# Exponentials one step later on ScalarE, softmax factors one step later on VectorE, in a two-layer attention kernel

## The chip, the cores and the metric

The kernel runs on one core of one Trainium2 chip. The metric is the device time of one execution in microseconds (us). The time before is 1312.04 us, the median of three runs (1309.96 to 1312.55).

## The reference, cut to what matters

Two layers, 512 tokens, width 1024, all in float32. Each layer runs two kinds of attention on the same normalised input, projects the joined result back and adds it, and then runs a feed-forward part with a short convolution:

```python
for l in range(DEPTH):                                   # 2 layers
    proj = rms_norm(x, attn_norm[l]) @ w_in[l]
    q_lat, kv_lat, k_rope, nsa_q, nsa_kv, gate_logits = jnp.split(proj, SPLIT_POINTS, axis=-1)
    o_mla = mla_attention(...)      # 8 heads, causal softmax
    o_nsa = nsa_attention(...)      # 8 heads, three gated branches:
                                    # compressed keys, selected keys, window
    x = x + jnp.concatenate([o_mla, o_nsa], axis=-1) @ w_out[l]
    x = x + conv_ffn(rms_norm(x, ffn_norm[l]), ...)
return rms_norm(x, final_norm)
```

The heart of each attention is `softmax(q k^T + mask) v`. With 512 tokens the selected and the window branch both come down to a causal softmax over all earlier tokens; the compressed branch is a small softmax over 31 pooled keys.

## The kernel before, in words

Every engine has its own program, with the order written out by hand, and semaphores tie the programs together. A layer is input projection, attention, output projection, feed-forward. The change is in the attention stage, which runs from about 104 to 250 us in layer 1 and from about 750 to 895 us in layer 2 of the profiled execution.

The stage is cut into 48 **units**: a unit is one block of 128 queries for one pair of heads and one branch. Four units (the blocks 2, 3, 0, 1, so with 384, 512, 128 and 256 keys) make a **group** g; groups 0 to 3 are the first kind of attention, 4 to 11 the second (its matmuls are L1631 and L1632, those of the first kind L1626). All engines walk through steps s = 0, 1, 2, ... and work on unit s - something in step s:

- TensorE in step s: transposes of the probabilities of unit s-3 (`turn`, L1645); then, in every fourth step, `spread(g)` (L1659), the transposes of the factors of group g, in step 4g+7; then the scores of unit s; in odd steps the products with the values for two units (L1692); and items from other work, among them `compressed` (L1704).
- VectorE in step s: adds the mask, takes the row maxima and writes the masked scores to SBUF (`row_max(s)`, L1193); the one-over-sum factors of a group (`factors(g)`, L1199, then L1204 or with gates L1208), in step 4g+5; the copy of the spread factors (`copy_factors`, L1219) in step 4g+7; `normalize` (L1226, L1230); `out_lo` (L1234); the low halves of other items (`item_lo`, L1245 and L1247), of the compressed branch (L1306 to L1320, L1261, L1267) and of the weights of the output projection (`split_lo`, L578) in steps 33, 37, 41 and 45.
- ScalarE in step s: copies unit s-3's transposed probabilities from PSUM to SBUF (`evac_turn`, L881 and L884 for the large blocks, L888 for the small); the exponentials of unit s (`exps(s)`, two activations of L870, each with the read of its sum); then other items: `evac_out` (L895), `item_hi` (L904 to L911), pieces of the compressed branch (L935 to L953, of which L938 and L949 wait for GpSimd) and the high halves of weights (`split_hi`, L571) in steps 32, 36, 40 and 44.

The transposes of the probabilities go to two PSUM banks in turn (3 and 4; from step 29 on also bank 5), and a large block takes both. So TensorE can transpose the next block only once ScalarE has copied the one before. TensorE's `turn(u)` waits for `exp_done` of unit u and for the copy that frees its bank; `spread(g)` waits for `fac_ready`, which `factors(g)` signals; `factors(g)` waits for the last exponentials of its group, unit 4g+3. `row_max(u)` waits until unit u-3 has been transposed, since three buffers hold the probabilities. The order within a step is what sets who waits behind whom:

```python
# ScalarE, L920 to L923
if 0 <= s - T_LAG < U: evac_turn(s - T_LAG)     # T_LAG = 3
if s < U: exps(s)
# VectorE, L1290 to L1296
if s < U: row_max(s)
if 0 <= s - 2 < U and (s - 2) % T == T - 1: factors((s - 2) // T)
```

Of the kernel before, what the change touches and what calls it, by code (L numbers as in the profile page):

```python
# [36 lines left out]
T = S // P  # L37
# [33 lines left out]
U = U_MLA + U_NSA  # L71
# [98 lines left out]
def at(s, l, n):  # L170

    return l * PER_LAYER[s.name] + (n + CREDIT.get(s.name, 0))
# [74 lines left out]
def hybrid_layers(nc, a, out):  # L247

    with ExitStack() as ctx:
# [337 lines left out]
        def unit(u):  # L587

            i, n = ORDER[u % T], u // T
            if u < U_MLA:  # L590
                return i, n, 0
            n -= U_MLA // T
            return i, H // 2 + n // 2, n % 2
# [151 lines left out]
        def _(act):  # L745
# [30 lines left out]
            for l in range(L):  # L776
# [78 lines left out]
                def evac_proj(kind, n, bank):  # L855

                    if kind == "k":
                        k_rows(n, bank)
                    if kind == "v":
                        v_rows(n, bank)  # L860
# [4 lines left out]
                def exps(u):  # L865
                    n = (unit(u)[0] + 1) * P
                    for h in range(2):
                        row = probs[:, u % 3, h, 0:n]
                        act.wait_ge(max_done, at(max_done, l, 2 * u + h + 1))
                        activate(row, row, ACT.Exp, scale=-1.0, bias=nmax[:, u % 4, h:h + 1],  # L870
                                 accum_out=rsum[:, u // T % 2, unit(u)[0], h:h + 1]).then_inc(exp_done, 1)
# [44 lines left out]
                for s in range(U + LAG + 2):  # L916
                    if s < len(STEP_PROJ):
                        for job in STEP_PROJ[s]:
                            evac_proj(*job)
                    if 0 <= s - T_LAG < U:  # L920
                        evac_turn(s - T_LAG)
                    if s < U:
                        exps(s)  # L923
                    if s == 2:
                        act.wait_ge(gate_in, at(gate_in, l, 1))
                        activate(gates[:, :, :], gate_e[:, :, :], ACT.Exp, scale=-1.0).then_inc(gate_exp, 1)
                    g = (s - LAG - 1) // T
                    if s > LAG and (s - LAG - 1) % T == T - 1:
                        if g < H // 2:
                            evac_out(g)  # L930
                    if s in ITEM_STEP:
                        item_hi(ITEM_STEP.index(s))
                    if s == HID_STEP:
                        act.wait_ge(cmp_used, at(cmp_used, l, 4))
                        activate(hid_rows, ps[:, HID_BANK, 0:CHID], ACT.Copy).then_inc(hid_out, 1)  # L935
                    if s == HIDT_STEP + 1:
                        act.wait_ge(gelu_in, at(gelu_in, l, 1))
                        activate(gelu_t, gelu_t, ACT.Exp, scale=-2.0 * (2.0 / np.pi) ** 0.5).then_inc(gelu_exp, 1)  # L938
                    if s == KVC_STEP:
                        act.wait_ge(kvc_acc, at(kvc_acc, l, 1))  # L940
                        activate(kc[:, :, :], ps[:, KVC_BANK, S - G * NCP:S].rearrange("p (g c) -> p g c", g=G), ACT.Copy)\
                            .then_inc(kch_done, 1)
                    if s in CS_STEP:
                        g = CS_STEP.index(s)
                        act.wait_ge(cs_acc, at(cs_acc, l, g + 1))
                        activate(cs_t[g], ps[:, CS_BANK[g], :], ACT.Copy).then_inc(cs_out, 1)
                    if s == CS_MAX_STEP + 1:
                        act.wait_ge(cs_sub, at(cs_sub, l, 1))
                        activate(scp, scp, ACT.Exp).then_inc(cs_exp, 1)  # L949
                    if s in PC_STEP:  # L950
                        g = PC_STEP.index(s)
                        act.wait_ge(pc_tp, at(pc_tp, l, g + 1))
                        activate(pct[:, g, :], ps[:, PC_BANK, :], ACT.Copy).then_inc(pct_ready, 1)  # L953
                    if s in WOUT_STEP:
                        split_hi(act, l, POS_WOUT + WOUT_STEP.index(s))
# [82 lines left out]
        def _(dve):  # L1038
# [47 lines left out]
            for l in range(L):  # L1086
# [129 lines left out]
                def copy_factors(g):  # L1216

                    dve.wait_ge(fac_done, at(fac_done, l, g + 1))
                    v.tensor_copy(onorm[:, g % 2, :], ps[:, FAC_BANK[g][0], :]).then_inc(fac_out, 1)  # L1219
# [61 lines left out]
                for s in range(U + LAG + 2):  # L1281
                    done = (s - LAG - 2) // T
                    closed = s >= LAG + 2 and (s - LAG - 2) % T == T - 1
                    if closed and done < H // 2:
                        out_lo(done)
                    if s > LAG + U_MLA and (s - LAG - 1 - U_MLA) % (2 * T) == 2 * T - 1:
                        add_compressed((s - LAG - 1 - U_MLA) // (2 * T))
                    if LAG <= s < U + LAG and (s - LAG) % T == T - 1:
                        copy_factors((s - LAG) // T)
                    if s < U:  # L1290
                        row_max(s)
                    if s < len(STEP_PROJ):
                        for job in STEP_PROJ[s]:
                            evac_proj(*job)
                    if 0 <= s - 2 < U and (s - 2) % T == T - 1:
                        factors((s - 2) // T)  # L1296
                    if s > LAG and (s - LAG - 1) % T == T - 1:
                        normalize((s - LAG - 1) // T)
                    if closed and done >= H // 2 and done % 2 == 1:
                        out_lo(H // 2 + (done - H // 2) // 2)  # L1300
                    if s - 1 in ITEM_STEP:
                        item_lo(ITEM_STEP.index(s - 1))
                    if s == HIDT_STEP + 1:
                        dve.wait_ge(hid_tp, at(hid_tp, l, 1))
                        pos = ps[:, HIDT_BANK, 0:2 * CMP_COLS].rearrange("p (a c) -> p a c", a=2)[:, :, 2 * NC]
                        tt(hid_b[:, :], pos, cols[:, C_B1:C_B1 + 2], ALU.add).then_inc(dve_chain, 1)  # L1306
                        dve.wait_ge(dve_chain, ch.next())
                        for kv in range(2):
                            c = kv * CMP_COLS
                            last = v.tensor_scalar(hid[:, kv, :, 0:NC],  # L1310
                                                   ps[:, HIDT_BANK, c:c + G * NC].rearrange("p (g c) -> p g c", g=G),
                                                   hid_b[:, kv:kv + 1], None, ALU.add)
                        last.then_inc(hid_in, 1)
                    if s == HIDT_STEP + 2:
                        dve.wait_ge(gelu_exp, at(gelu_exp, l, 1))
                        v.tensor_scalar(gelu_t, gelu_t, 1.0, None, ALU.add).then_inc(dve_chain, 1)
                        dve.wait_ge(dve_chain, ch.next())
                        v.reciprocal(gelu_t, gelu_t).then_inc(dve_chain, 1)
                        dve.wait_ge(dve_chain, ch.next())
                        tt(hid_flat, hid_flat, gelu_t, ALU.mult).then_inc(hid_ready, 1)  # L1320
                    if s == KVC_STEP + 1:
                        dve.wait_ge(kch_done, at(kch_done, l, 1))
                        v.tensor_copy(v_cmp[:, :, :], ps[:, KVC_BANK, 0:G * HD].rearrange("p (g c) -> p g c", g=G))\
                            .then_inc(kvc_ready, 1)
                    if s - 1 in BACK_STEP:
                        cs_mask(BACK_STEP.index(s - 1))
                    if s == CS_MAX_STEP:
                        cs_less_max()
                    if s == CS_SCALE_STEP:
                        cs_scale()  # L1330
                    if s == 3:
                        dve.wait_ge(gate_exp, at(gate_exp, l, 1))
                        v.tensor_scalar(gates[:, :, :], gates[:, :, :], 1.0, None, ALU.add).then_inc(dve_chain, 1)
                        dve.wait_ge(dve_chain, ch.next())
                        v.reciprocal(gates[:, :, :], gates[:, :, :]).then_inc(gates_ready, 1)
                    if s - 1 in WOUT_STEP:
                        split_lo(dve, l, POS_WOUT + WOUT_STEP.index(s - 1))
# [659 lines left out]
```

## Time and profile before

| | |
|---|---|
| median of 3 runs | 1312.04 us |
| the profiled execution's own time | 1311.85 us |
| its span, first to last instruction | 1310.1 us |
| TensorE matmuls busy | 1267.1 us, 97% |
| TensorE weight loads busy | 1045.5 us, 80% |
| VectorE busy | 700.1 us, 53% |
| ScalarE busy | 639.3 us, 49% |
| mean granted TensorE clock | 0.994 |

Busy times are sums over the instructions of an engine. Matmuls are pipelined and their ends are modelled, so a busy share of 97% is not a TensorE at its peak; where TensorE shows as idle, it was waiting. The clock is given as a share of full speed. The chain of work that ended last is 85% TensorE, 8% VectorE and 4% ScalarE.

### The profile page before, as it was taken

How to read it: one execution, taken by the hardware profiler on the slowest of the kernel's cores; microseconds unless marked ns; L12 is line 12 of the kernel's file. 1: busy time of each engine (PE TensorE's matmuls, PEld its weight loads, DVE VectorE, ACT ScalarE, POOL GpSimd, SP SyncE). 2: the span in 40 equal slices, each digit the busy share in tenths (PEclk: the TensorE clock that was granted, in tenths of full speed). 3: DMA queues.
4: the chain of work that ended last, by engine and by line, in shares of the span. 5: the costliest groups of instructions: out<-in, count | busy, mean ns of one | idle time of the engine just before them, and what ended most of it. 6: DMA issues, size and time to landing. Idle time of an engine off the chain costs nothing.

```text
span 1310.1 us, 18479 instructions
## 1 busy us (share of the span) xinstructions
PE 1267.1 (97%) x6612; PEld 1045.5 (80%) x6612; DVE 700.1 (53%) x1216; ACT 639.3 (49%) x1191; POOL 70.7 (5%) x161
## 2 busy tenths in 40 slices
PE   8999989999999999999999999899999999999997
PEld 7997667788888888888889866667888888888886
DVE  5435778455555555533363457782655555554334
ACT  4336788344444444322352468782454444443223
POOL 2013110000000000000010311100000000000000
PEclk9999999999999999999999999999999999999999
DMA  6420101124333333332143210012223333333211
GB/s 205 125 89 1 66 1 49 42 72 120 97 96 99 97 97 99 105 98 97 45 121 94 65 65 1 1 57 86 76 75 97 97 97 96 98 105 114 96 64 65
DMA packets 121003, 107.05 MB, mean 82 GB/s; under 512 B 3763, under 2 KB 110485, under 8 KB 120946
## 3 DMA queue, kind: packets, MB, share of 16 engines
q1 hardware_dynamic: 118912, 101.13, 25.3%
q0 software_dynamic: 1456, 3.52, 0.9%
q10 hardware_dynamic: 578, 1.64, 0.3%
q8 instruction: 35, 0.57, 0.2%
q14 instruction: 22, 0.18, 0.0%
HBM read 104.19 MB, written 2.10 MB: 81 GB/s over the span
## 4 chain that ended last, share of the span: by engine, by line
PE 85%; DVE 8%; ACT 4%; issue 2%; POOL 1%; DMA 1%; DVEq 0%; ACTq 0%; POOLq 0%
PE ps L1449 24%; PE ps L1451 24%; PE ps L1450 24%; PE ps L1645 3%; PE ps L1692 3%; DVE probs L1193 2%; PE ps L1626 2%; ACT probs L870 1%; PE ps L1632 1%; PE ps L1631 1%; DVE probs L1066 1%; DVE w_lo L578 1%; DVE x L1084 1%; PE ps L1659 1%; PE ps L1704 1%
## 5 line engine op out<-in xcount | busy, mean ns | idle before, releaser
L1449 PE MATMUL ps<-ht_hi,w_hi 128*128 128x512 f32 (+2 forms) x776 | 297.2, 383 | 2.5 <-DVE w_lo L578 2.5
L1451 PE MATMUL ps<-ht_hi,w_lo 128*128 128x512 f32 (+2 forms) x776 | 295.9, 381 | 0.0
L1450 PE MATMUL ps<-ht_lo,w_hi 128*128 128x512 f32 (+2 forms) x776 | 295.8, 381 | 0.0
L578 DVE TENSOR_TENSOR w_lo<-raw,w_hi 128x1024 fp32r<-128x1024 f32 (+4 forms) x196 | 218.7, 1140 | 95.0 <-ACT w_hi L571 86.7
L571 ACT ACTIVATE w_hi<-raw 128x1024 fp32r<-128x1024 f32 (+4 forms) x196 | 187.2, 982 | 107.9 <-PE ps L1451 107.6
L1365 DVE SCALAR_TENSOR_TENSOR conv<-ps,cols,conv 128x510 f32<-128x510 f32 (+1 forms) x176 | 127.6, 746 | 179.7 <-ACT conv L978 173.9
L1449 PEld LDWEIGHTS ps<-ht_hi,w_hi 128*128 128x128 f32 x776 | 145.9, 188 | 30.8 <-DVE w_lo L578 3.0
L1450 PEld LDWEIGHTS ps<-ht_lo,w_hi 128*128 128x128 f32 x776 | 145.9, 188 | 28.0 <-issue 0.5
L1451 PEld LDWEIGHTS ps<-ht_hi,w_lo 128*128 128x128 f32 x776 | 145.9, 188 | 27.8
L1449 PE MATMUL ps<-w_hi,ht_hi 128*128 128x430 f32 (+1 forms) x392 | 147.3, 376 | 3.7 <-DVE w_lo L578 2.0
L978 ACT ACTIVATE conv<-ps,cols 128x512 f32<-128x512 f32 x88 | 68.1, 774 | 159.9 <-PE ps L1451 159.7
L1451 PE MATMUL ps<-w_hi,ht_lo 128*128 128x430 f32 (+1 forms) x392 | 144.5, 369 | 0.0
L1450 PE MATMUL ps<-w_lo,ht_hi 128*128 128x430 f32 (+1 forms) x392 | 144.4, 368 | 0.0
L1449 PE MATMUL ps<-w_hi,g_hi 128*128 128x512 f32 x352 | 137.2, 390 | 0.8 <-DVE g_all L1373 0.8
L1450 PE MATMUL ps<-w_lo,g_hi 128*128 128x512 f32 x352 | 137.0, 389 | 0.0
L1451 PE MATMUL ps<-w_hi,g_lo 128*128 128x512 f32 x352 | 136.9, 389 | 0.0
L870 ACT ACTIVATE probs<-probs,nmax 128x384 f32<-128x384 f32 (+1 forms) x192 | 106.2, 556 | 31.1 <-DVE nmax L1193 30.5
L1193 DVE CUSTOM_DVE_ANT_0 probs<-ps,causal 128x384 f32<-128x384 f32 (+1 forms) x192 | 87.1, 487 | 50.2 <-PE ps L1626 25.0
L997 ACT ACTIVATE g_hi<-g_all 128x512 fp32r (+1 forms) x44 | 27.6, 630 | 149.8 <-PE ps L1451 149.8
L1386 DVE TENSOR_TENSOR g_lo<-g_all,g_hi 128x512 fp32r<-128x512 f32 x44 | 30.3, 691 | 129.8 <-ACT g_hi L997 129.8
L1645 PE MATMUL ps<-ident,probs 128*128 128x128 f32 x480 | 72.5, 278 | 21.6 <-ACT probs_t L881 12.0
L1449 PEld LDWEIGHTS ps<-w_hi,ht_hi 128*128 128x128 f32 x392 | 73.9, 189 | 12.2 <-DVE w_lo L578 2.6
(193 smaller groups left out, 1510.7 us busy)
## 6 DMA issues: line engine op xcount, KB each, us to landing
raw<-in_ffn_w_up_dram SPq DMA_DIRECT2D x88, 512.0 KB, 4.1
raw<-in_ffn_w_down_dram SPq DMA_DIRECT2D x44, 512.0 KB, 3.3
raw<-in_w_in_dram SPq DMA_DIRECT2D x32, 430.0 KB, 4.3
raw<-in_w_out_dram SPq DMA_DIRECT2D x16, 512.0 KB, 3.4
raw<-in_nsa_cmp_w_dram SPq DMA_DIRECT2D x8, 512.0 KB, 3.7
x<-in_x_dram ACTq DMA_DIRECT2D x3, 512.0 KB, 8.1
raw<-in_mla_w_uq_dram SPq DMA_DIRECT2D x4, 384.0 KB, 2.9
out_dram<-x SPq DMA_DIRECT2D x3, 512.0 KB, 2.6
```

The source lines that it names most:

```text
L571: last = nc.scalar.activation(d(w_hi)[:, :, d0:d1], r(raw)[:, :, r0:r1], ACT.Copy)
L578: last = nc.vector.tensor_tensor(d(w_lo)[:, :, d0:d1], r(raw)[:, :, r0:r1], d(w_hi)[:, :, d0:d1].bitcast(F32), ALU.subtract)
L870: activate(row, row, ACT.Exp, scale=-1.0, bias=nmax[:, u % 4, h:h + 1], accum_out=rsum[:, u // T % 2, unit(u)[0], h:h + 1]).then_inc(exp_d ...
L978: activate(conv[:, fl, uv, :], ps[:, 4 * fl + uv, :], ACT.Identity, bias=bias, scale=tap)\
L1193: v.tensor_tensor_reduce(probs[:, u % 3, h, 0:n], score_place(u, h), causal[:, S - n:S], -1.0, -NEG, ALU.add, ALU.min, nmax[:, u % 4, h:h ...
L1365: ins = stt(out=conv[:, fl, uv, back:S], in0=ps[:, 4 * fl + uv, 0:S - back], scalar=c, in1=conv[:, fl, uv, back:S], op0=ALU.mult, op1=ALU.add)
L1386: tt(g_lo[:, n % 2, :].unsqueeze(1), g_all[:, bass.ds(k, 1), :], g_hi[:, n % 2, :].unsqueeze(1).bitcast(F32), ALU.subtract).then_inc(gl_do ...
L1449: mm(o, lhs[0], rhs[0], start=start, stop=False)
L1450: mm(o, lhs[0], rhs[1], start=False, stop=False)
L1451: return mm(o, lhs[1], rhs[0], start=False, stop=stop)
L1645: last = nc.tensor.transpose(ps[:, bank, c0 + b * P:c0 + (b + 1) * P], probs[:, u % 3, h, b * P:(b + 1) * P], ident[:, :])
L1692: last = mm(ps[64 * h:64 * h + VD, out_bank(g), q0 + q:q0 + 2 * P], w, pt_half(u)[:, h, b, q:2 * P], start=b == 0, stop=b == n - 1)
```

## The change

ScalarE runs the exponentials of unit s-1 in step s, where it ran those of unit s; they still come behind that step's copy of transposed probabilities. The pass through step 48 takes in the last unit. VectorE's factors of a group move from step 4g+5, behind the row maxima, to step 4g+6, ahead of them, since the exponentials that they wait for now come a step later.

```diff
@@ ScalarE, the loop over steps
                     if 0 <= s - T_LAG < U:
                         evac_turn(s - T_LAG)
-                    if s < U:
-                        exps(s)
+                    if 1 <= s <= U:
+                        exps(s - 1)
                     if s == 2:
@@ VectorE, the loop over steps
                     if LAG <= s < U + LAG and (s - LAG) % T == T - 1:
                         copy_factors((s - LAG) // T)
+                    if 0 <= s - 3 < U and (s - 3) % T == T - 1:
+                        factors((s - 3) // T)
                     if s < U:
                         row_max(s)
                     if s < len(STEP_PROJ):
                         for job in STEP_PROJ[s]:
                             evac_proj(*job)
-                    if 0 <= s - 2 < U and (s - 2) % T == T - 1:
-                        factors((s - 2) // T)
```

## Rows read from the trace of the kernel before

**Rows 1.** Waits, layer 1's attention: who waited; us in total, times, longest

```profile
PE ps L1645 <- ACT probs_t L881: 6.0, 5, 2.6
PE ps L1645 <- ACT probs_t L888: 4.8, 4, 2.4
...
PE ps L1847 <- DVE qs L1247: 0.5, 1, 0.5
```

**Rows 2.** Timeline of TensorE: start, length, work, idle before it and its releaser

```profile
142.13 0.52 PE L1645 MATMUL ps<-ident,probs 128*128 128x128 f32 x3 [2.37 <-ACT probs_t L888]
...
182.91 1.06 PE L1645 MATMUL ps<-ident,probs 128*128 128x128 f32 x8 [2.58 <-ACT probs_t L881]
...
219.39 0.63 PE L1645 MATMUL ps<-ident,probs 128*128 128x128 f32 x4 [0.81 <-ACT probs_t L881]
...
237.31 1.06 PE L1645 MATMUL ps<-ident,probs 128*128 128x128 f32 x8 [1.39 <-ACT probs_t L881]
```

**Rows 3.** Timeline of ScalarE, exponentials of 512 and of 128 keys

```profile
214.59 0.72 ACT L870 ACTIVATE probs<-probs,nmax 128x512 f32<-128x512 f32 x1
...
217.99 0.40 ACT L870 ACTIVATE probs<-probs,nmax 128x128 f32<-128x128 f32 x1 [1.40 <-DVE nmax L1193]
```

**Rows 4.** Timeline of VectorE, ends of groups 6, 7 and 8

```profile
198.39 0.69 DVE L1208 TENSOR_TENSOR onorm<-fac,gates 128x512 f32<-128x512 f32 x1
...
205.60 0.69 DVE L1208 TENSOR_TENSOR onorm<-fac,gates 128x512 f32<-128x512 f32 x1
...
215.31 0.69 DVE L1208 TENSOR_TENSOR onorm<-fac,gates 128x512 f32<-128x512 f32 x1
215.93 0.68 DVE L1234 TENSOR_TENSOR ht_lo<-onorm,ht_hi 128x512 fp32r<-128x512 f32 x1
216.53 1.22 DVE L578 TENSOR_TENSOR w_lo<-raw,w_hi 128x1024 fp32r<-128x1024 f32 x1
217.66 0.28 DVE L1193 CUSTOM_DVE_ANT_0 probs<-ps,causal 128x128 f32<-128x128 f32 x1
```

**Rows 5.** Timeline of TensorE, the spreads of groups 6, 7 and 8

```profile
199.14 0.66 PE L1659 MATMUL ps<-ident,onorm 128*128 128x128 f32 x4
...
207.10 0.60 PE L1659 MATMUL ps<-ident,onorm 128*128 128x128 f32 x4
...
216.06 0.66 PE L1659 MATMUL ps<-ident,onorm 128*128 128x128 f32 x4
```

**Rows 6.** Timeline of VectorE, factors of group 1 and what follows them

```profile
137.43 0.20 DVE L1199 RECIPROCAL fac<-rsum 128x8 f32<-128x8 f32 x1
...
138.00 0.15 DVE L1306 TENSOR_TENSOR hid_b<-ps,cols 128x2 f32<-128x2 f32 x1
```

**Rows 7.** Timeline, the compressed branch's chain in steps 21 to 23

```profile
176.45 0.20 DVE L1199 RECIPROCAL fac<-rsum 128x8 f32<-128x8 f32 x1
...
177.29 0.68 DVE L1261 TENSOR_TENSOR vm<-ps,cmask 128x512 f32<-128x512 f32 x1
178.01 1.22 DVE L1267 TENSOR_REDUCE cstat<-vm 128x32 f32<-128x1024 f32 x1
...
179.38 1.91 POOL L726 TENSOR_TENSOR vm<-vm,cstat 128x1024 f32<-128x1024 f32 x1 [8.81 <-DVE cstat L1267]
...
181.33 1.06 ACT L949 ACTIVATE vm<-vm 128x1024 f32<-128x1024 f32 x1 [0.98 <-POOL vm L726]
```

**Rows 8.** Windows: stretch, length, busy TensorE, loads, VectorE, ScalarE, GpSimd, then granted clock

```profile
144.00:145.00 1.00, 1.00 (x5) 0.51 (x6) 0.86 (x4) 0.74 (x3) 0.00 (x0) 0.50 0.00 0
...
831.00:832.00 1.00, 1.00 (x4) 0.80 (x3) 0.79 (x3) 1.00 (x5) 0.95 (x1) 0.50 0.00 0
```

**Rows 9.** Timeline of TensorE, the same work in layer 1 and layer 2

```profile
187.68 0.66 PE L1864 MATMUL ps<-ident,vm 128*128 128x128 f32 x4
...
828.37 1.06 PE L1645 MATMUL ps<-ident,probs 128*128 128x128 f32 x8 [2.58 <-ACT probs_t L881]
...
834.41 0.65 PE L1864 MATMUL ps<-ident,vm 128*128 128x128 f32 x4
```

## The prediction

> **What bounds the kernel now.** I read the share of busy time first: TensorE stands at 97% of the span, so the change can only win time in which TensorE waits. The chain that ended last says the same (85% TensorE). Then I looked for the waits in the attention stage, since the diff touches nothing else. The reader should see that in layer 1's stage TensorE waits 11.3 us in ten places, and that nine of them, 10.8 us, end on ScalarE's copies L881 and L888; the tenth is VectorE's L1247 [rows 1]. The timeline gives the places: one of 2.37, one of 2.58, one of 0.81, one of 1.39 [rows 2]. Layer 2 repeats them (its 2.58 stands in [rows 9]). So some 22 us of 1310 are the most that ScalarE's order could be worth. What keeps a copy late is seen on ScalarE's own timeline: in step 38 it sat 1.40 us until VectorE had the maxima of the unit whose exponentials stood first [rows 3]. The copy of step 39, which TensorE wanted at 218.6, stood behind them.
>
> **ScalarE's part.** Nothing is added: 192 activations of L870 stay, each group of exponentials is only taken one place later, when its maxima are long there. That removes the wait of [rows 3] and its like. The price is slack: turn(u) on TensorE then finds its exponentials one step instead of two steps old. Four steps of TensorE are 8.96 us (207.10 to 216.06) [rows 5], 2.2 a step, and the two largest exponentials are 0.72 each [rows 3], so I cost it at nothing; if ScalarE were full it would be a wait of up to 1.4. The two waits in the second half of a stage, 0.81 and 1.39 idle, go [rows 2]. I take 1.0 and 1.5 for them, since a gap is longer than its idle by the end of a pipelined matmul; **-2.5 a layer**.
>
> **Waits that stay.** The 2.37 is not ScalarE's order: the copy stands behind L938, which waits for GpSimd, which waits for VectorE's L1310. The 2.58 is the same with L949 [rows 2, 7]. There the other half of the diff helps. In step 9 factors(1) ran ahead of L1306 and took 0.57 [rows 6]; it now comes behind, so that chain is 0.6 earlier. The 0.5 on L1247 goes in the same way, as its step 13 has factors too [rows 1]. So TensorE and all behind it is 1.1 early at step 21. There factors(4) took 0.84 between the maxima and the sum and maximum of the compressed branch (176.45 to 177.29) [rows 7], and it leaves too; about 0.2 more comes from the copy L895 that VectorE waited for. The chain L1267, GpSimd's L726, ScalarE's L949, copy L881 [rows 7] is therefore 2.1 early, and with it the transposes at 182.91 [rows 2]: **-2.1 a layer**. The small waits of L888 and L881 between do go, but nothing is added for them: GpSimd's chain sets the time of 182.91 whatever TensorE does before it.
>
> **VectorE's part, the cost.** In the second half of the stage factors(g) moves from behind the maxima of step 4g+5 to the start of step 4g+6. In the text of the loop it also moves behind everything else of step 4g+5: out_lo, 0.60 (215.93 to 216.53), and split_lo, 1.13 (216.53 to 217.66) [rows 4]. TensorE's spread(g) in step 4g+7 waits for it, and the two rows show how close: for group 6 L1208 ends at 198.39 + 0.69 = 199.08 and the spread starts at 199.14, slack none; for group 8 it is 216.00 against 216.06, slack none; for group 7 206.29 against 207.10, slack 0.75 after a latency of 0.06 [rows 4, 5]. So:
> - group 6, step 29 has out_lo alone: +0.60
> - group 7, step 33 has split_lo alone: 1.13 - 0.75 = +0.38
> - group 8, step 37 has both: 0.60 + 1.13 = +1.73
> - groups 9 and 10 repeat 7 and 8: +0.38, +1.73
>
> Sum **+4.8 a layer**. VectorE's work here is timed by TensorE's scores a few steps earlier, so an early stage moves both and the slack stays. Queued behind the factors on VectorE is only row_max(4g+6), whose start does not change in these groups. The wait of spread(g) holds up the scores behind it by as much. The copy L1219 comes later with it, and only normalize(g) needs that, in the next step.
>
> **The clock.** In layer 2 TensorE's granted clock fell to 0.50, the 1.2 GHz level, for some 3 us after the gap of 2.58 [rows 8, 9]. The same work, from the transposes after the gap to L1864, took 4.77 us in layer 1 (182.91 to 187.68), where the clock held, and 6.04 in layer 2 (828.37 to 834.41) [rows 2, 9]: a fall costs 1.27. There are three falls in the two stages, the others after the gap of 2.37 in each layer (that of layer 1 is in [rows 8]). A fall after a gap depends on more than its length, as these two of 2.58 show. Bounds: all three go, -3.8; none goes and the four new gaps of 1.7 each bring one, +5.1. Gaps up to 1.39 brought none [rows 2]. I take one fall gone, that of layer 2's 2.58, since that gap is cut up: **-1.3**.
> The Trainium skill (TensorE: Matmul & The Clock Gate, A second HAM failure mode: psum-queue depth-cycling) says that frequent short idles between groups of matmuls can themselves make the clock swing between its levels. By that rule the new short gaps would cost as well, which is the rival on the slow side below; the trace, with its gaps of 0.81 and 1.39 at full clock, so far speaks against it.
>
> **Sum.** Per layer -2.5 - 2.1 + 4.8 = +0.2, two layers +0.4, clock -1.3: 1311.85 - 0.9 = 1310.95 against the profiled execution. That execution lies 0.2 under the median of 1312.04, so I say 1311.2. The ends: every hand-off above is good to 0.5 a layer in the chain of GpSimd and 0.2 in the spreads; with that alone 1309.5 to 1313.8. A measurement of this kernel can tell about 0.2%, 2.6 us.
>
> **Rivals.**
> - B, all three falls of the clock go: the gaps of 2.37 and 2.58 become about 1.8 and 1.0, and near these the trace shows none. 1312.04 + 0.4 - 3.8 = 1308.6. Against it: the gap at step 23 may only be cut in two. 22%.
> - C, the spreads cost nothing, since VectorE gets through its step sooner than I think and TensorE comes later: -2.5 - 2.1 a layer and -1.3 for the clock, 1312.04 - 9.2 - 1.3 = 1301.5. Against it: slack none in two of three rows. 8%.
> - D, slower: TensorE's clock. Each new gap of 1.7 before the spreads of groups 8 and 10, in both layers, is followed by a fall, and no old one goes: 1312.04 + 0.4 + 4 x 1.27 = 1317.5. It decides from the second new fall on. For it: one gap of 2.58 had a fall and one had not. Against: 1.39 never had. 14%.
> - E, the half of the diff on ScalarE doesn't do what it says where it matters most: L895 or the chain over GpSimd waits for VectorE as late as before, the transposes at 182.91 stay where they are, and the cost of the spreads is all there: 2 x (4.8 - 2.5) = +4.6, 1316.6. For it: L895 now stands where no exponential covers its wait for normalize. 10%.
> - My case A: 46%.
>
> **How the numbers follow.** Of A's 46%, 5 lie under 1309.4, 2 over 1314.7. Faster: 22 + 8 + 5 = 35%. Slower: 14 + 10 + 2 = 26%. Within 0.2%: 39%. The range 1306.0 to 1317.0 takes in A, B and E and a part of D; A's own is 1309.5 to 1313.8.
>
> **What would show it.** Right: ScalarE's idle before L870 that L1193 ends falls to a few tenths a group; the waits of L1645 on L881 and L888 in the second half of the stage are gone; L1659 or its weight load now waits for VectorE's L1208, in groups 8 and 10 by some 1.5 us, in 4 as well; L938 and L949 still wait for GpSimd, the one 0.6 and the other some 2 us earlier. Wrong: if L1659 shows no wait, C holds; if the granted clock is at half after such a wait, D; if the transposes after L949 come no earlier, E. The feed-forward part and the projections should not move by themselves at all.

## Result, and the profile after

| | median | runs | ratio to before, 95% interval |
|---|---|---|---|
| before | 1311.18 us | 15, 1309.56 to 1312.90 | |
| after | 1315.60 us | 15, 1312.48 to 1318.78 | 1.0035 [1.0028, 1.0042] |

The change costs 4.4 us, where 0.8 was forecast as a gain (against the median of 1312.04 shown then) and no measurable difference as the likeliest. The profiled execution after has a span of 1316.9 us and an own time of 1318.78, the slowest of its 15 runs, so its span is not set against that of before. It is read below by stretches of its stage.

The page of the kernel after, shares and the costliest groups (busy time, mean ns of one | idle of the engine before them, and what ended most of it):

```profile
PE 1273.6 (97%) x6612; PEld 1050.8 (80%) x6612; DVE 702.9 (53%) x1216; ACT 637.9 (48%) x1191; POOL 72.2 (5%) x161
...
L870 ACT ACTIVATE probs<-probs,nmax 128x384 f32<-128x384 f32 (+1 forms) x192 | 105.8, 557 | 0.4
...
L1645 PE MATMUL ps<-ident,probs 128*128 128x128 f32 x480 | 73.2, 282 | 8.4 <-ACT probs_t L888 6.1
```

TensorE is as much the bound as before. ScalarE no longer waits ahead of an exponential: 0.4 us in the whole program, the 1.40 of [rows 3] is gone. That half of the change did what it says. The waits in layer 1's attention, kernel after (who waited for whom: us in total, times, longest), answer to [rows 1]:

```profile
PEld ps L1659 <- DVE onorm L1208: 7.1, 6, 1.9
PE ps L1659 <- DVE onorm L1208: 5.7, 6, 1.6
...
PE ps L1645 <- ACT probs_t L888: 3.0, 2, 2.2
ACT vm L949 <- POOL vm L726: 2.6, 1, 2.6
ACT ht_hi L895 <- DVE onorm L1226: 2.3, 3, 0.9
...
PE ps L1645 <- ACT probs_t L881: 1.6, 3, 0.9
PE ps L1659 <- DVE onorm L1204: 1.6, 1, 1.6
```

L1645's waits on ScalarE's copies fell from 10.8 us to 4.6. In their place stand waits that the kernel before did not have: the spreads L1659 on VectorE's factors, 5.7 + 1.6 = 7.3 us. The timeline of TensorE after, layer 1 (start, length, work, idle before it and what ended it), has them one by one and answers to [rows 2, 5]:

```profile
168.34 0.66 PE L1659 MATMUL ps<-ident,onorm 128*128 128x128 f32 x4 [1.55 <-DVE onorm L1204]
...
179.24 0.66 PE L1659 MATMUL ps<-ident,onorm 128*128 128x128 f32 x4 [1.59 <-DVE onorm L1208]
...
182.57 1.94 PE L1645 MATMUL ps<-ident,probs 128*128 128x128 f32 x8 [0.86 <-ACT probs_t L881]
...
193.11 1.07 PE L1704 MATMUL ps<-vm,v_cmp 32*64 32x512 f32 x4 [0.24 <-ACT vm L953]
...
201.67 0.66 PE L1659 MATMUL ps<-ident,onorm 128*128 128x128 f32 x4 [0.48 <-DVE onorm L1208]
...
210.01 0.66 PE L1659 MATMUL ps<-ident,onorm 128*128 128x128 f32 x4 [0.21 <-DVE onorm L1208]
...
220.77 0.66 PE L1659 MATMUL ps<-ident,onorm 128*128 128x128 f32 x4 [1.62 <-DVE onorm L1208]
...
229.11 0.66 PE L1659 MATMUL ps<-ident,onorm 128*128 128x128 f32 x4 [0.21 <-DVE onorm L1208]
...
239.87 0.66 PE L1659 MATMUL ps<-ident,onorm 128*128 128x128 f32 x4 [1.62 <-DVE onorm L1208]
```

The last five are spread(6) to spread(10), which the forecast had priced. The first two are spread(3) and spread(4), which it had not; it named a wait in group 4 among its signs, and none in group 3. The transposes at 182.57 are only 0.34 earlier than before, where 2.1 was forecast. Why spread(3) waits is seen on VectorE and GpSimd. The kernel before:

```profile
166.55 0.43 DVE L1204 COPY onorm<-fac 128x512 f32<-128x512 f32 x1
166.89 1.38 DVE L1245 TENSOR_TENSOR ks<-ps,ks 64x512 fp32r<-64x512 f32 x2
```

and the kernel after (VectorE, with GpSimd's row between):

```profile
165.42 1.39 DVE L1245 TENSOR_TENSOR ks<-ps,ks 64x512 fp32r<-64x512 f32 x2
166.84 0.20 DVE L1199 RECIPROCAL fac<-rsum 128x8 f32<-128x8 f32 x1
...
166.97 2.21 POOL L718 CAST ks<-ks 64x1024 fp32r<-64x1024 f32 x2 [23.80 <-DVE ks L1245]
...
167.08 1.21 DVE L1204 COPY onorm<-fac 128x512 f32<-128x512 f32 x1
```

The factors of group 3 now stand behind item_lo (L1245, 1.39), and they land beside the cast L718 that item_lo has just released on GpSimd: the same copy takes 1.21 instead of 0.43. It ends at 168.29, and the spread starts at 168.34.

**Stretches.** From here the stage is measured from spread to spread on TensorE, in us: "(0) to (2)" runs from the start of spread(0) to the start of spread(2). Each value is from the profiled execution, from a layer whose stretch had no fall of the granted clock, or it says so. The last column is twice the sum of the three stretches less twice that of before. The variants are described under Experiments; "late 1, 2, 4" has the factors of these groups alone in the new, later place.

| kernel | (0) to (2) | (2) to (5) | (5) to (11) | two layers |
|---|---|---|---|---|
| before | 29.88 (31.49 less a fall of 1.61) | 33.12 | 58.88 | |
| after | 28.99 (30.60 less a fall) | 33.50 | 61.71 | +4.6 |
| ScalarE's half alone | 29.83 | 32.00 | 57.54 | -5.0 |
| VectorE's half alone | 29.04 | 33.80 | 61.62 | +5.2 |
| late 1, 2, 4 | 28.99 | 31.70 | 57.52 | -7.3 |
| late 0 to 5 | 28.99 | 33.71 (with a fall) | 57.54 | -3.3 |
| group 3 early | 29.00 (30.61 less a fall) | 31.70 | 61.69 | +1.0 |
| split later | 28.99 | 33.48 | 58.74 | -1.3 |
| cast waits | 28.97 | 32.70 | 61.71 | +3.0 |

The price of a fall comes from "late 1, 2, 4": spread(0) to spread(2) took 28.99 in layer 1 at full clock and 30.60 in layer 2, where the clock fell, so 1.61. The two layers of ScalarE's half alone (29.83 and 31.45) and of "cast waits" (28.97 and 30.57) give 1.62 and 1.60. The 33.50 of after is from layer 2, whose short fall at 829 shows in no time: "split later", with the same order up to there, took 33.48 without one. In layer 1, with some 7 us at half clock, the kernel after took 35.64.

### The profile page after: what moved, and what is told of

It reads as the page before. It is cut to its first block, busy times and chain, and to the rows that moved or that the text cites. A ratio compares the mean times of both kernels' runs of the same rounds, so it can differ in the third digit from the quotient of the medians.

```text
span 1316.9 us, 18479 instructions
## 1 busy us (share of the span) xinstructions
PE 1273.6 (97%) x6612; PEld 1050.8 (80%) x6612; DVE 702.9 (53%) x1216; ACT 637.9 (48%) x1191; POOL 72.2 (5%) x161
## 4 chain that ended last, share of the span: by engine, by line
PE 84%; DVE 10%; ACT 3%; issue 2%; POOL 0%; DMA 0%; DVEq 0%; POOLq 0%; ACTq 0%
PE ps L1449 24%; PE ps L1450 24%; PE ps L1451 24%; PE ps L1692 3%; PE ps L1645 2%; DVE probs L1193 2%; PE ps L1626 2%; DVE w_lo L578 1%; PE ps L1659 1%; DVE probs L1066 1%; DVE onorm L1226 1%; DVE x L1084 1%; PE ps L1631 1%; PE ps L1632 1%; PE ps L1704 1%
## 5 line engine op out<-in xcount | busy, mean ns | idle before, releaser
L1449 PE MATMUL ps<-ht_hi,w_hi 128*128 128x512 f32 (+2 forms) x776 | 298.0, 384 | 2.5 <-DVE w_lo L578 2.5
L578 DVE TENSOR_TENSOR w_lo<-raw,w_hi 128x1024 fp32r<-128x1024 f32 (+4 forms) x196 | 218.7, 1140 | 95.2 <-ACT w_hi L571 87.3
L1449 PEld LDWEIGHTS ps<-ht_hi,w_hi 128*128 128x128 f32 x776 | 146.5, 189 | 31.0 <-DVE w_lo L578 2.9
L1449 PE MATMUL ps<-w_hi,ht_hi 128*128 128x430 f32 (+1 forms) x392 | 147.6, 377 | 2.4 <-DVE w_lo L578 1.3
L1449 PE MATMUL ps<-w_hi,g_hi 128*128 128x512 f32 x352 | 137.3, 390 | 0.8 <-DVE g_all L1373 0.8
L1449 PEld LDWEIGHTS ps<-w_hi,ht_hi 128*128 128x128 f32 x392 | 74.2, 189 | 10.6 <-DVE w_lo L578 1.9
L1645 PE MATMUL ps<-ident,probs 128*128 128x128 f32 x480 | 73.2, 282 | 8.4 <-ACT probs_t L888 6.1
```

Of the source, the lines that this page charges most:

```text
L578: last = nc.vector.tensor_tensor(d(w_lo)[:, :, d0:d1], r(raw)[:, :, r0:r1], d(w_hi)[:, :, d0:d1].bitcast(F32), ALU.subtract)
L1449: mm(o, lhs[0], rhs[0], start=start, stop=False)
L1645: last = nc.tensor.transpose(ps[:, bank, c0 + b * P:c0 + (b + 1) * P], probs[:, u % 3, h, b * P:(b + 1) * P], ident[:, :])
```

## Experiments

Each ratio below is to the kernel before as it ran beside that variant: 1311.82 us, 14 runs, for the first four variants (the two halves, late 1, 2, 4 and late 0 to 5), 1310.91 us, 27 runs, for the others. The variants have 5 to 11 runs each.

Three theories. **T1**: the loss is the factors' new place on VectorE; ScalarE's half gains. **R1**: ScalarE's move costs by itself, since L895 now waits 2.3 us for VectorE with no exponential to cover it. **R2**: the order matters little, and the 4.4 us are falls of TensorE's clock.

### ScalarE's half alone

```diff
 # against the kernel before
-                    if s < U:
-                        exps(s)
+                    if 1 <= s <= U:
+                        exps(s - 1)
```

> ScalarE's half of the change alone: exponentials one place later, VectorE's factors where they were. T1 (what is lost, the factors lose, by their new place on VectorE): about 1304.5 us, 6.5 under the kernel before; the spreads of groups 6 to 10 wait for nothing of VectorE's, spread(6) to spread(8) are 16.9 us apart, and TensorE's gaps of 0.81 and 1.39 in the second half of a stage are gone. R1 (ScalarE's move costs too, by L895 or L953 waiting where no exponential covers it): 1311 or more. R2 (the loss is falls of TensorE's clock and neither half's order): the time goes with the granted clock, within 1 us of the kernel before at an equal clock.

Measured 1307.94 us, ratio 0.9973 [0.9963, 0.9983]: 3.9 faster, and as much at equal clock (below). R1 and R2 fall: this half gains. But it gains less than the 6.5 that T1 gave. Its timeline of TensorE:

```profile
180.44 1.06 PE L1645 MATMUL ps<-ident,probs 128*128 128x128 f32 x8 [3.51 <-ACT probs_t L881]
...
188.82 1.07 PE L1704 MATMUL ps<-vm,v_cmp 32*64 32x512 f32 x4 [0.25 <-ACT vm L953]
...
234.10 0.50 PE L1449 MATMUL ps<-w_hi,ht_hi 128*128 128x512 f32 x1 [0.49 <-DVE nmax L1193]
```

TensorE is early at step 23 and then stands 3.51 us before the transposes that end GpSimd's chain. L1704 is 0.31 later by the new order of ScalarE (spread(5) to spread(6) takes 9.28 instead of 8.97, the one cost of this half that shows). And where 1.39 of [rows 2] goes, L1449 runs into VectorE's maxima: of the 1.4 us of gain only 0.67 is left. Over the second half of the stage it gains 1.34, not 2.5.

### VectorE's half alone

```diff
 # against the kernel after
-                    if 1 <= s <= U:
-                        exps(s - 1)
+                    if s < U:
+                        exps(s)
```

> VectorE's half alone: the factors at the head of the next step, ScalarE's exponentials where they were. T1: the spreads' delays of 4.9 us a layer are all there and ScalarE's stalls of 0.81 and 1.39 too, unless TensorE's wait at the spread takes their place; 1316 to 1319 us. R1 (the loss is ScalarE's): about 1311. R2: the kernel before's time at an equal clock.

Measured 1316.78 us, ratio 1.0040 [1.0027, 1.0053]. The whole loss is there without ScalarE's half, and in its late stretch (61.62) ScalarE's stalls have vanished in the wait of the spreads. T1 holds, R1 is out. The two halves do not add: on top of VectorE's half, ScalarE's takes (0) to (2) from 29.04 to 28.99, (2) to (5) from 33.80 to 33.50 and (5) to (11) from 61.62 to 61.71, some 0.5 us in two layers, where alone it takes 5.0 off them.

### Late factors for groups 1, 2 and 4 only

```diff
 # against the kernel after
-                    if 0 <= s - 3 < U and (s - 3) % T == T - 1:
+                    if 0 <= s - 3 < U and (s - 3) % T == T - 1 and (s - 3) // T in (1, 2, 4):
                         factors((s - 3) // T)
...
+                    if 0 <= s - 2 < U and (s - 2) % T == T - 1 and (s - 2) // T not in (1, 2, 4):
+                        factors((s - 2) // T)
```

> The changed kernel with the late factors for groups 1, 2 and 4 alone (where they stood ahead of GpSimd's chain and of L1247), all others where they were. T1: the delays of spread(3) and spread(6) to spread(10) go, the gains in the first half stay: about 1303 us, the best of these four. R1: 1310 or more. If the late factors of the first half are worth nothing either, it comes out as ScalarE's half alone, within 1 us.

Measured 1301.60 us, ratio 0.9930 [0.9918, 0.9942]: 10.2 us faster than before, 14 than the change as made, and the best kernel here. Expected were about 1303. Late factors in groups 1 and 2 are worth 0.84 a layer (29.83 to 28.99), where 1.1 was forecast. Before spread(5) two waits are left (timeline of TensorE, its lines two below those of before):

```profile
175.42 0.66 PE L1661 MATMUL ps<-ident,onorm 128*128 128x128 f32 x4 [1.59 <-DVE onorm L1208]
...
178.75 1.06 PE L1647 MATMUL ps<-ident,probs 128*128 128x128 f32 x8 [1.40 <-ACT probs_t L881]
```

The transposes come 178.75 - 125.13 = 53.6 us after spread(0). In the kernel before it was 182.91 - 125.56 = 57.35 with a fall in between, 55.7 without. So they are 2.1 early here, the size of the forecast's early gain, once group 3 is out of it. With ScalarE's half alone they come 180.44 - 125.67 = 54.8 after spread(0), 1.0 early; so that half has 1.0 of the 2.1, and the late factors have 1.1.

### Late factors in groups 0 to 5, then in all but group 3

Against the kernel after, with the old place as in the diff above for the groups not named, first the one and then the other:

```diff
+                    if 0 <= s - 3 < U and (s - 3) % T == T - 1 and (s - 3) // T in (0, 1, 2, 3, 4, 5):
...
+                    if 0 <= s - 3 < U and (s - 3) % T == T - 1 and (s - 3) // T in (0, 1, 2, 4, 5, 6, 7, 8, 9, 10, 11):
```

> The changed kernel with late factors in groups 0 to 5 alone, groups 6 to 11 where they were. T1: 4.8 us a layer less than the changed kernel, 1306; spread(3) is still late by 1.4. R1 and R2: as the changed kernel, 1314 to 1316.

> The changed kernel with the factors of group 3 alone back in their old place, ahead of item_lo. T1 (spread(3) waits for factors that now stand behind item_lo's two parts of 0.69 and beside GpSimd's cast L718): L1204 takes 0.43 again instead of 1.21, spread(2) to spread(4) falls from 23.1 to 21.3 us as in the kernel with groups 1, 2 and 4 late, some 1.8 a layer: about 1312 us. Rival (the transposes of step 23 are set by GpSimd's chain, which hides all of it): 1315 to 1316, as the changed kernel.

Measured: groups 0 to 5 late, 1304.34 us, 0.9953 [0.9935, 0.9972]. With the second half of the stage as in ScalarE's half alone (57.54 against 61.71), 11.3 us of the change as made come back, where T1 said 9 to 10. The stretches explain 7.9 of them; the remainder lies in the clock or outside the stretches and was not traced, and the 6 runs spread from 1302.56 to 1310.32. All but group 3 late, 1309.70 us, 0.9993 [0.9984, 1.0002], against 1315.60 with it. The stretch (2) to (5) falls from 33.50 to 31.70: 1.8 a layer, as expected. Its L1204 takes 0.43, ahead of L1245. About 1312 was expected. At equal clock (below) this kernel is 3.2 under the kernel after, near the 2 x 1.8 of the stretch; the remaining 2.7 of the 5.9 between the medians go with its higher mean clock (0.9965 against 0.9937).

### GpSimd's cast held back

One wait more on GpSimd, ahead of its second pair of casts: they start only once `factors(3)` is done.

```diff
 # against the kernel after
+                pool.wait_ge(fac_ready, at(fac_ready, l, 4))
                 twice(1)
```

> The changed kernel with one wait more on GpSimd: its second cast L718 starts behind the factors of group 3, so that L1204 has the SBUF to itself. If the cast beside it stretches L1204: 0.43 instead of 1.21, and spread(3) 0.8 earlier, TensorE's wait there 0.8 instead of 1.55; the transposes of step 23 come by what GpSimd's chain lets through, 0 to 0.8 a layer, 1314 to 1315.6 in all. Rival (the copy is longer by its place behind L1245 or by its own data): 1.2 as before and spread(3) where it was.

Timelines of this kernel (its lines from L723 on stand one below those of after), VectorE, TensorE and GpSimd:

```profile
167.42 0.43 DVE L1205 COPY onorm<-fac 128x512 f32<-128x512 f32 x1
...
167.90 0.66 PE L1660 MATMUL ps<-ident,onorm 128*128 128x128 f32 x4 [0.78 <-DVE onorm L1205]
...
168.00 2.13 POOL L718 CAST ks<-ks 64x1024 fp32r<-64x1024 f32 x2 [24.58 <-DVE onorm L1205]
```

The copy takes 0.43 behind L1245 as well, and TensorE waits 0.78 instead of 1.55. So of the late spread(3) half is item_lo ahead of the factors and half the cast beside them. The time, 1311.63 us (1.0004 [0.9995, 1.0013]), is 4.0 under the kernel after and under the 1314 to 1315.6 expected, though the stage explains 2 x 0.8 only. The rest goes with the clock: its 11 runs show 0.994 to 0.999 of full clock, the kernel after 0.991 to 0.997, and at equal clock the two are 1.4 apart.

### w_out's split a step later

```diff
 # against the kernel after
-                    if s - 1 in WOUT_STEP:
-                        split_lo(dve, l, POS_WOUT + WOUT_STEP.index(s - 1))
+                    if s - 2 in WOUT_STEP:
+                        split_lo(dve, l, POS_WOUT + WOUT_STEP.index(s - 2))
```

> The changed kernel with VectorE's split_lo of w_out one step later, so that the factors of groups 7 to 10 no longer stand behind its 1.13. T1: spread(7) and spread(9) wait for nothing of VectorE's, spread(8) and spread(10) 0.6 instead of 1.6, spread(5) to spread(11) falls from 61.7 to about 58.3 us: about 1309. Rival (it is the place one step on, not what stands ahead of the factors there): the gaps of 1.6 stay, 1315 to 1316.

Measured 1308.64 us, ratio 0.9985 [0.9976, 0.9994]; (5) to (11) took 58.74, where about 58.3 was expected. Its spreads 7 and 8, timeline of TensorE:

```profile
205.92 0.60 PE L1659 MATMUL ps<-ident,onorm 128*128 128x128 f32 x4
...
215.48 0.66 PE L1659 MATMUL ps<-ident,onorm 128*128 128x128 f32 x4 [0.49 <-DVE onorm L1208]
```

Spread(7) waits for nothing, spread(8) for out_lo alone. Against 210.01 and 220.77 of after it is L578 ahead of the factors, and not the later place as such, that made the 1.6 us waits.

### Late factors for groups 1 and 2 only

```diff
 # against the kernel after; the other groups are back in the old place
+                    if 0 <= s - 3 < U and (s - 3) % T == T - 1 and (s - 3) // T in (1, 2):
                         factors((s - 3) // T)
```

> Late factors for groups 1 and 2 alone, ScalarE's half in. The factors of group 4, late, run beside GpSimd's L726 and hold up spread(4) by 1.6, early they hold up L1267 and so L726 and L949. If the late place is right for group 4: spread(2) to spread(5) 32.0 instead of 31.7 us without a fall of the clock, 1302.2. If it is the wrong one: 31 or less, 1300.

Measured 1304.15 us, ratio 0.9950 [0.9936, 0.9963], 5 runs. Falls of the clock in both layers (mean 0.992 to 0.994) lie in the stretch in question, so its time tells nothing. The start of the transposes of step 23 in layer 1 does, since TensorE stood waiting for ScalarE's copy when the clock fell there (timeline of TensorE):

```profile
179.92 1.94 PE L1647 MATMUL ps<-ident,probs 128*128 128x128 f32 x8 [3.51 <-ACT probs_t L881]
```

It comes 24.93 us after spread(2) (154.99 to 179.92), against 24.63 with group 4 late (154.12 to 178.75). Late is right for group 4, but by 0.3, not the 0.84 that it takes out of the way, because L726 then runs beside L1208 and takes 2.46 instead of 1.91. That holds in all ten kernels: L726 takes 2.45 to 2.46 in the seven that have group 4 late, and 1.91 in the three that have it early.

## Why the forecast was wrong

**ScalarE's part, -2.5 a layer in the second half.** The number came out, by luck: in the changed kernel spread(8) to (9) lost 1.0 and spread(10) to (11) 1.43, beside the delays. The reason given did not hold. ScalarE's half alone recovers 0.98 and 0.67, less the 0.31 at L1704, so 1.34: VectorE's maxima hold back the other 0.76 of the 1.43. And VectorE's half, without ScalarE's, loses the same 1.43 (15.06 to 13.63): a TensorE that stands 1.6 at spread(10) no longer meets the late copy. Costing the slack at nothing was nearly right: the one price seen is the 0.31 at L1704, which the sum did not have.

**VectorE's cost, +4.8 a layer.** Right to 0.15: the spreads of groups 6 to 10 came +0.60, +0.38, +1.80, +0.38, +1.79 later, sum 4.95. These are the distances from spread to spread less those of before, with the 0.31 and the gains of 1.0 and 1.43 taken apart; for spread(9) that takes the +0.38 of spread(7) again (8.34 against 8.96). Behind spread(8) VectorE's timeline of after shows the queue that [rows 4] let one see:

```profile
218.05 0.69 DVE L1234 TENSOR_TENSOR ht_lo<-onorm,ht_hi 128x512 fp32r<-128x512 f32 x1
218.65 1.22 DVE L578 TENSOR_TENSOR w_lo<-raw,w_hi 128x1024 fp32r<-128x1024 f32 x1
219.79 0.20 DVE L1199 RECIPROCAL fac<-rsum 128x8 f32<-128x8 f32 x1
220.02 0.69 DVE L1208 TENSOR_TENSOR onorm<-fac,gates 128x512 f32<-128x512 f32 x1
```

So (5) to (11) is 4.95 - 2.43 + 0.31 = +2.83 a layer, 58.88 to 61.71, where 2.3 was forecast.

**The step that failed: the early gain, -2.1 a layer**, "the chain ... is therefore 2.1 early". It came out as 0.5 by spread(5) (29.88 + 33.12 = 63.0 before, 62.5 after). The size of 2.1 was there to be had, as "late 1, 2, 4" shows, though in other parts: groups 1 and 2 gave 0.84 (1.1 forecast), group 4 gave 0.3 (0.84), and ScalarE's half 1.0 (0.2, since the small waits of L888 and L881 were given nothing). The mistake that made the loss is that the cost of the moved factors was looked for in the second half of the stage only. In step 17 factors(3) is moved past item_lo just as factors(7) is moved past split_lo: 1.39, and 0.78 more because the cast L718 starts there. Group 3 costs 33.50 - 31.70 = 1.8 a layer; without it ("late 1, 2, 4") spread(5) is 2.3 early (60.7 against 63.0), with it 0.5. "GpSimd's chain sets the time of 182.91 whatever TensorE does before it" was wrong both ways. TensorE's early start in ScalarE's half alone moved the chain 1.0 earlier, and a late spread(3) moves it later: "group 3 early" against the kernel after shows that.

The parts add up so: in two layers the early gain came 3.2 short, the second half cost 1.1 more, and the clock 1.8 more (0.5 lost for 1.3 gained), 6.1 in all. The miss is 5.3, a loss of 4.4 for the 0.9 that the sum gained. The 0.8 between them was not traced; 0.7 of it is what the stretches give above the cost at equal clock (4.6 against 3.9, below).

**Contention.** The parts of the forecast that took VectorE's work out of GpSimd's way did not ask what GpSimd would now meet. VectorE and GpSimd after, with ScalarE's L949 last, answer to [rows 7]:

```profile
177.12 1.22 DVE L1267 TENSOR_REDUCE cstat<-vm 128x32 f32<-128x1024 f32 x1
...
178.49 0.69 DVE L1208 TENSOR_TENSOR onorm<-fac,gates 128x512 f32<-128x512 f32 x1
...
178.50 2.46 POOL L726 TENSOR_TENSOR vm<-vm,cstat 128x1024 f32<-128x1024 f32 x1 [9.32 <-DVE cstat L1267]
...
180.99 1.06 ACT L949 ACTIVATE vm<-vm 128x1024 f32<-128x1024 f32 x1 [2.61 <-POOL vm L726]
```

L1267 is 0.89 earlier, L949 only 0.34: L726 lost 0.55 beside L1208, which takes 0.61 there until the next instruction starts. The Trainium skill (SBUF — State Buffer, SBUF: two separate sides) says that VectorE and GpSimd share a pair of ports as an exclusive lock, which VectorE takes for an operation in a two-port mode or with two SBUF inputs, and that whichever starts first holds it for the whole instruction while the other blocks. The traces agree in their lengths: L1208 has two SBUF inputs, and L726, which starts within 0.01 us of it, is longer by about L1208's length. Of L718's two casts the first started 0.11 ahead of L1204 and took 1.09; L1204 ended 0.23 after it. Which of L1208 and L726 came first the profile cannot tell, since its times on GpSimd are rough.

**The clock, -1.3.** Wrong in sign: it cost about 0.5 (the 4.4 between the medians less 3.9 at equal clock, below). The profiled execution of before had three falls in the two stages [rows 8], and the price of 1.27 holds at its place: (2) to (5) took 33.12 in layer 1 and 34.39 in layer 2. That of after had some 3 us at half after 142, some 7 after 180, and again after 791, 829 and 948. Windows of the kernel after (the granted clock is the third number from the end):

```profile
144.00:145.00 1.00, 1.00 (x5) 0.53 (x6) 0.82 (x4) 0.98 (x4) 0.00 (x0) 0.50 0.00 0
...
183.00:184.00 1.00, 1.00 (x7) 1.00 (x6) 0.90 (x4) 0.88 (x5) 0.00 (x0) 0.50 0.00 0
...
830.00:831.00 1.00, 1.00 (x7) 0.78 (x7) 0.69 (x1) 0.30 (x1) 0.67 (x1) 0.50 0.00 0
```

Over its 15 runs time goes with the mean clock, 1312.5 us at 0.997 and 1317.4 to 1318.8 at 0.991. So the runs of one kernel spread by 5 us with the clock, but the order of the work is what moved the median: a line through all runs of all ten kernels, with one slope (0.88 us for 0.001 of clock), puts the kernel after 3.9 us above before at equal clock, VectorE's half alone 4.1 above, ScalarE's half alone 3.9 below, "late 1, 2, 4" 8.0 below. The last column of the stretches is within 0.7 of such figures for four variants, within 1.2 for three, and 2.6 off for late 0 to 5 (-3.3 against -5.9). One slope does not know that a fall costs much in one place and little in another, so the differences of 1 us and more stay open.

The rival on the clock said 1317.5, but the new gaps that it priced, of 1.62 at 220.77 and 239.87, brought no fall in either layer. The new gap of 1.59 before spread(4) did: in the kernel after the clock fell within some 1.3 us of its end in layer 1 and at once in layer 2 (the fall at 829). The fall in layer 2 cost nothing that shows (33.50 against 33.48), the long one in layer 1 some 2.1 (35.64).

**The rivals.** Nearest was E, the early gain that doesn't come, 1316.6 at 10%. It named L895 or GpSimd's chain as late; what was late was the spread before them.

## What to carry over

- An instruction group moved across a step boundary moves past everything that stands there in any iteration, not in the ones looked at. List, for each iteration of the loop, what it is moved past, before adding up; here group 3 was the one left out, and with it in its old place the change makes no measurable difference (0.9993) instead of a loss.
- Where a moved piece gains in some iterations and loses in others, move it in those alone: late in groups 1, 2 and 4 gave 1301.60 us against 1315.60 and 1311.82.
- When a gain frees VectorE beside GpSimd, see what GpSimd's operation then runs beside.

## What was not expected of the hardware

- A copy from SBUF to SBUF on VectorE took 1.21 us beside a GpSimd cast and 0.43 with the cast held back; a tensor_tensor on GpSimd (L726) took 2.46 beside a VectorE operation with two SBUF inputs, and 1.91 beside maxima and a copy read from PSUM.
- The same gap is not the same fall of the clock. Before the transposes of step 23, 3.51 us in ScalarE's half alone brought none in layer 1 and 3.50 brought one in layer 2; with groups 1 and 2 late the clock fell in both layers within the gap of 3.51. The gap of about 2.15 at step 9 (141.82 in the kernel after) stands in seven kernels: in layer 1 three of them had a fall behind it (after, group 3 early, cast waits) and four had none. What decides it stays open; a fall cost 1.6 us between spread(0) and spread(2), and 0 to 0.2 where it lay ahead of the wait for GpSimd's chain (with groups 0 to 5 late 33.71 and 33.76, in layer 2 of the kernel after 33.50, against 33.48 without a fall).
